# A hybrid backbone step with sixteen experts: the last two experts one behind the other instead of interleaved

## The reference

```python
def moe_ffn(x, w_router, router_bias, w_gate, w_up, w_down):
    ...
    h = jax.nn.silu(jnp.einsum("td,edf->tef", t, w_gate)) * jnp.einsum("td,edf->tef", t, w_up)
    h = h * gates.astype(h.dtype)[..., None]
    return jnp.einsum("tef,efd->td", h, w_down).reshape(B, L, D)
...
    x = x + g2 * moe_ffn(h, P["w_router"], P["router_bias"], P["w_gate"][l], P["w_up"][l], P["w_down"][l])
```

## Time and profile before

| | us |
|---|---|
| median of 3 runs | 661.88 |
| lowest, highest | 661.65, 663.79 |
| the profiled execution | 664.11 |
| its span, first to last instruction | 662.3 |
| TensorE busy in the span | 563.9 (85%) |
| VectorE, ScalarE, GpSimd busy | 246.3, 137.8, 66.2 |
| DMA queue of the weights, share of 16 engines | 60.6% |
| granted TensorE clock, mean | 0.945 |

### The profile page before, as it was taken

The page is one execution under the profiler, slowest core; times in us unless marked ns, Lnnn a source line. Parts: engine busy times, 40 slices in busy tenths (PEclk is TensorE's granted clock), DMA queues, the critical chain, the costliest instruction groups (busy, mean ns, idle before and its releaser), DMA issues.

```text
span 662.3 us, 13154 instructions
## 1 busy us (share of the span) xinstructions
PE 563.9 (85%) x5670; PEld 367.7 (56%) x5670; DVE 246.3 (37%) x526; ACT 137.8 (21%) x260; POOL 66.2 (10%) x98
## 2 busy tenths in 40 slices
PE   2789999999999899599964899999777777867974
PEld 0575544566675566574443799997344444434531
DVE  2551648887736824720358611011000000001025
ACT  1330562422128601010141111000000000000012
POOL 1039000000003100020002000000000000300031
PEclk9989999999999999899977699999999999979988
DMA  8989830303110914961597599999999999999972
GB/s 265 392 300 368 308 128 0 128 1 127 55 74 10 374 72 153 356 176 63 190 406 279 187 353 387 398 384 389 393 396 395 395 396 396 394 365 412 405 273 100
DMA packets 79277, 176.16 MB, mean 266 GB/s; under 512 B 6072, under 2 KB 11199, under 8 KB 78847
## 3 DMA queue, kind: packets, MB, share of 16 engines
q1 hardware_dynamic: 64848, 149.01, 60.6%
q0 software_dynamic: 6032, 18.75, 8.3%
q10 hardware_dynamic: 8351, 7.73, 3.5%
HBM read 163.01 MB, written 12.47 MB: 265 GB/s over the span
## 4 chain that ended last, share of the span: by engine, by line
PE 23%; SPq 19%; DMA 8%; issue 4%; DVE 2%; ACT 1%; POOL 1%; ACTq 0%; DVEq 0%; POOLq 0%
SPq L1091 17%; PE psum L874 6%; PE psum L799 5%; PE psum L871 4%; DMA slot<-in_w_down 3%; PE psum L882 2%; PE psum L806 2%; SPq L1105 2%; DMA y_rows<-ye 1%; DMA h_rows<-ye 1%; DMA slot<-y_rows,rows 1%; DMA xe<-h_rows,lst 1%; PE psum L813 1%; POOL slot L1244 1%; PE psum L459 1%
## 5 line engine op out<-in xcount | busy, mean ns | idle before, releaser
L882 PE MATMUL psum<-slot,xeTa 128*32 128x256 f32 x1536 | 98.9, 415 | 28.8 <-DMA slot<-in_w_gate 25.3
L547 PE MATMUL psum<-hT,slot 128*128 128x384 f32 x304 | 100.8, 489 | 0.0
L882 PEld LDWEIGHTS psum<-slot,xeTa 128*32 128x32 f32 x1536 | 57.4, 119 | 69.7 <-issue 28.8
L547 PEld LDWEIGHTS psum<-hT,slot 128*128 128x128 f32 x304 | 56.9, 190 | 38.2
L882 PE MATMUL psum<-slot,heT 128*32 128x256 f32 x768 | 45.3, 389 | 6.3 <-DMA slot<-in_w_down 6.3
L871 PE MATMUL psum<-slot,xeTa 128*32 128x384 f32 x384 | 44.8, 509 | 0.5 <-ACT xeTa L1542 0.5
L874 PE MATMUL psum<-slot,xeTa 128*32 128x128 f32 x384 | 45.3, 282 | 0.0
L874 PEld LDWEIGHTS psum<-slot,xeTa 128*32 128x32 f32 x384 | 43.4, 114 | 0.6
L556 PE MATMUL psum<-slot,hT 128*128 128x512 f32 x96 | 42.3, 596 | 1.1 <-DMA slot<-in_w_in 1.1
L2214 DVE COPY heT<-psum 128x256 f32<-128x256 f32 (+1 forms) x16 | 7.3, 457 | 95.8 <-PE psum L902 95.8
L1550 ACT ACTIVATE he<-psum 128x256 f32<-128x256 f32 (+1 forms) x16 | 6.6, 410 | 154.9 <-PE psum L882 126.9
(11 more groups left out here) (429 smaller groups left out, 774.8 us busy)
## 6 DMA issues: line engine op xcount, KB each, us to landing
slot<-in_w_gate SPq DMA_DIRECT2D x16, 2048.0 KB, 23.2
slot<-in_w_up SPq DMA_DIRECT2D x16, 2048.0 KB, 18.8
slot<-in_w_down SPq DMA_DIRECT2D x16, 2048.0 KB, 19.7
slot<-in_w_ada SPq DMA_DIRECT2D x12, 2048.0 KB, 15.4
slot<-in_w_in SPq DMA_DIRECT2D x7, 2048.0 KB, 9.0
y_rows<-T POOLq DMA_DIRECT2D x11, 384.0 KB, 15.4
slot<-in_w_out SPq DMA_DIRECT2D x2, 2048.0 KB, 16.3
y_rows<-ye ACTq DMA_DIRECT2D x22, 128.0 KB, 6.8
```

What stands on the lines that cost most here:

```text
L547: last = mm(o[:, 0:TOK], w[:, kt, tile(i)], hT[:, kt, :], start=(kt == 0), stop=(kt == KT - 1))
L882: last = mm(psum[32 * c:32 * c + 32, bank, 0:HALF], x(k, c % 2), w(k)[:, c // 2 * HALF:c // 2 * HALF + HALF], start=(k == 0), stop=(k == t ...
```

## The change

The last pair is worked one position behind the other. On TensorE, gate of position 15 and the carry of tile 0 move from between up(14) and turn_h(14) to behind down(14). On SyncE, the load of down(14) comes ahead of the load of gate(15). On ScalarE, silu of position 15 comes behind the copy and the writes of position 14's result.

```diff
@@ TensorE, experts()
                     up(p, 3, slot[home(p, 1)], n).then_inc(s["up_done"], 1)
-                    if not (last_pair and p == 1):
+                    if not last_pair:
                         pe.wait_ge(s["g_silu"], n + 1)
-                        if last_pair:
-                            pe.wait_ge(s["lists"], 2)
-                            pe.wait_ge(s["xt_ready"], E)
-                            carry(0, 0)
-                            carry(0, 1)
                         gate(n + 1, 1 - p, it + p)
...
                     down(1, w, n).then_inc(s["down_done"], 1)
+                    if last_pair and p == 0:
+                        pe.wait_ge(s["lists"], 2)
+                        pe.wait_ge(s["xt_ready"], E)
+                        carry(0, 0)
+                        carry(0, 1)
+                        gate(E - 1, 1, it)
@@ SyncE
             reload(E - 2, 0, 1, E // 2 - 1)
+            reload(E - 2, 0, 2, E // 2 - 1)
             reload(E - 1, 1, 0, E // 2 - 1)
-            reload(E - 2, 0, 2, E // 2 - 1)
             reload(E - 1, 1, 1, E // 2 - 1)
@@ ScalarE, experts()
-                    if not (last_pair and p == 1):
+                    if not last_pair:
                         gate_silu(n + 1, 1 - p, not (first and p == 0))
+                    elif p == 1:
+                        gate_silu(n, p, True)
```

## The result

| | before | changed |
|---|---|---|
| median, 20 runs each, us | 661.93 | 665.26 |
| lowest, highest | 660.12, 666.31 | 663.10, 669.65 |
| ratio, 95% interval | | 1.0051 (1.0034 to 1.0068) |
| span of the profiled execution | 662.3 | 665.6 |

The account below looks back on a forecast made before the run. TensorE's own string, 0.88 us behind the gathers' chain, was taken to bound the tail. Down15 +1.24, wait -0.88, queue 0: +0.36, rounded to +0.4, giving 662.3 us; own range 661.3 to 663.5, with rivals 660.3 to 664.6.

Parts of the forecast that it names:

- What bounds: Kernel's tail: weights stream until the last slab; behind it TensorE's own string is only 0.88 us behind the gathers' chain.
- SyncE's wait for down 12: SyncE's slab loads: down14 waits for down_done of position 12, up to 1.5 us late at the issuer, costing 0.
- TensorE's string, +1.24: Up14 to down15's end: exposed multiply (0.68 us) and silu (about 0.55) make down15 end 1.24 us later.
- The write and the gathers: Position 14's writes go out earlier, gathers start 3 to 5 us earlier, and the 0.88 us wait goes.
- margin of 1.3 us: Down15's start on TensorE: its slab was given 1.3 us to spare, called thin.
- rival of starved weights: Earlier gathers slow down15's slab: 663.7 us at half share, 665.3 at three quarters; chance 0.18.
- Behind down15: TensorE's 3.31 us gap from a 4.71 us branch moves with down15 and keeps its length.
- The clock: Ident products behind the gap stay at the lower clock, 3.03 us against 1.98; rival of no fall: -1.05 us, chance 0.08.

Follow-up runs that it names:

- a_act_as_before: Changed kernel with ScalarE's part undone: silu of position 15 again ahead of the copy and writes of position 14; ratio to before 1.0023.
- a_carry1_late: Changed kernel with the ident products of tile 1 moved from ahead of up15 to behind it; ratio to before 1.0049.
- a_again: The changed kernel once more, unedited, for a second profile; median 667.50 us, ratio to before 1.0067.
- a_gathers_ht15: Changed kernel with GpSimd also waiting for heT of position 15 ahead of the gathers; ratio to before 1.0016.

## Why the prediction was wrong

- **What bounds: right.** The gathers' chain had 0.88 us over TensorE's own string and no more; once down15 came later, nothing waited for it, and the changed kernel's closing sums run in one piece. The edit that puts the jump behind the closing sums shows it from the other side: there the last tile waits for the gathers' chain again, 1.44 us.
- **SyncE's wait for down 12: right, 0.** Down14 was issued at 595.92, its product began at 617.68 without a wait for it, and with the writes held back the slabs of up15 and down15 land as early as before (15.7 and 21.1 us behind up14).
- **TensorE's string, +1.24: right, and hidden under the slab.** Each step up to the turn of h15 came within 0.1 us, and where the slab is in time (`a_act_as_before`) down15 starts 1.23 us later than before. But in the changed kernel the slabs of up15 and down15 landed later than in the kernel before, so that giving silu and multiply their cover back gained nothing that the median shows (`a_carry1_late`).
- **"The write and the gathers": the step that put position 14's write only to the gathers' account failed.** The writes are transfers too, and put ahead of the last slab, with the gain behind them, they made it late, 22.9 instead of 20.9 us behind up14. Down15 so started 0.75 us behind its heT, and the margin of 1.3 us that the prediction gave this slab was gone. (The writes themselves took 7.7 us, so the first gather came at 631.80, at the late end of the 628.4 to 631.5 given.) The rival of starved weights had the symptom right, its cause was wrong: the gathers moved no slab.
- **"Behind down15": the step that failed most.** I took the branch's 4.71 us as fixed to its place because "the traffic in that gap is the gathers' in both kernels". It is 3.4 to 3.7 us without traffic, and what counts is whether the gathers are in full run when the fetch starts: they led it by 1.7 us before, by 5.8 after, and the code's packet came 4.0 us behind the branch's start instead of 2.3. That is +1.66 us in the gap. The prediction said itself that the stall can grow with DMA traffic, but this had no number in the sum and no chance; it should have been a rival of its own.
- **The clock: kept, and moved.** The ident products took 3.78 us instead of 3.03 (+0.76 from start to start), but the Y15 products behind them less (3.44 instead of 3.87 us, -0.43), since the low clock ended earlier in them. With the wait of 0.88 us that went, this is the -0.55 behind the gap.

In the sum: forecast +1.24 - 0.88 = +0.36. Measured in the profiles: +0.15 shift ahead of the tail, +1.32 string, +0.75 slab, +1.66 branch, -0.55 behind it: +3.33. With the gathers' start put back beside down15 the kernel came to 1.0016, near the forecast's 1.0006. That is the branch's part taken back and not the forecast's own sum: down15 was late there too, the ident products ran at the upper clock, and TensorE waited for VectorE and for the gathers' chain (1.79 and 0.70 us).

## What to carry to other kernels

Work that is started earlier "for nothing" also moves its transfers earlier, and these run into what was quiet before: price each transfer that moves against the last load and against code fetches, not only against the one who waits for it. The gap with "issue" as releaser behind a taken branch was a DMA in disguise here; look for packets of the instruction queue and for the traffic at its start, and if possible lay the usual case straight behind the loop and jump afterwards. A transfer chain that ended last isn't worth more than its lead over the next engine's own string, here 0.88 us.

## What the runs showed beyond that

TensorE can pause inside straight code as well: three profiles of the changed kernel and its variants have down15 cut once or twice by "issue" gaps of 0.73 to 0.82 us while gathers run (the rows of `a_again` above), two more have cuts of 0.33 to 0.34, and none of the four profiles with the order of before has one. In each of the five an instruction packet is recorded 0.4 to 1.2 us ahead of the first cut. Whether late code makes the cuts isn't shown: such packets fall into down15 without a cut too, at 634.35 in the kernel before.

And VectorE's Y15 multiply started 2.6 to 5.6 us behind down15's end in five of the sixteen profiles, with "remote" as releaser; in the others 0.1 us behind it. In three of the five the jump's gap covered this. In the kernel before without the If (down15 ends at 635.13) it didn't:

```profile
640.57 1.29 DVE L2246 TENSOR_TENSOR G<-psum,hT 128x512 f32<-128x512 f32 x2 [9.59 <-remote]
```

TensorE then waited 4.87 us for it, and 1.79 us in `a_gathers_ht15`. What delays VectorE stays open; its own code coming late was my guess, but in this profile no instruction packet is recorded between 632.5 and 643.0. It may be why taking away the If gained the kernel before nothing where the closing sums ahead of the jump gained it 1.5 us. In the changed kernel without the If, VectorE's multiply for h15 came 1.6 us late in the same way (TensorE waited 2.21 us instead of 0.61).
